# A semaphore for each part of a block's rows in the expert phase of a decoder step

## The reference, cut to what matters

```python
def expert_block(args):
    toks, e = args
    xb = x_pad[toks]
    hb = jax.nn.silu(xb @ w1[e]) * (xb @ w3[e])
    return hb @ w2[e]

out = lax.map(expert_block, (row_tok.reshape(n_blocks, EXPERT_BLOCK), block_expert))
```

## Time and profile before

| what | value |
| --- | --- |
| median of 3 runs | 2936.85 us (2933.5 to 2942.09) |
| the profiled execution | 2944.2 us, its span 2942.7 us |
| mean granted TensorE clock | 0.955 |
| TensorE busy | 2629.6 us, 89% of the span |
| HBM read, written | 460.86 MB, 112.29 MB |
| experts: first hidden product to last output product | about 1848 to 2848 us |

### The profile page before, as it was taken

One profiled execution on the slowest core, in us unless ns is written; L12 is line 12 of the kernel. 1 busy time (PEld: TensorE's weight loads), 2 busy tenths in 40 slices (PEclk: granted clock), 3 DMA queues, 4 the chain that ended last, 5 costly groups with the idle time before them and its releaser, 6 DMA issues. The chain is left out here.

```text
span 2942.7 us, 63889 instructions
## 1 busy us (share of the span) xinstructions
PE 2629.6 (89%) x23589; PEld 1367.6 (46%) x23589; DVE 1380.8 (47%) x2816; ACT 1049.8 (36%) x1938; POOL 646.5 (22%) x914
## 2 busy tenths in 40 slices
PE   7999999976988898998989997788889997788888
PEld 3444444433544444554535554454445554454443
DVE  2241414143877787887867776122222221122218
ACT  2222222113777777777842221211111211111114
POOL 0101010101112111211201223333233332233343
PEclk8999999997999999999999998899999999899989
DMA  8020201146667676766763344887977879979737
GB/s 321 15 86 15 83 17 67 47 150 221 212 223 265 224 245 222 253 214 227 249 224 104 129 145 150 247 259 224 292 224 219 245 232 322 308 215 277 240 110 316
DMA packets 296450, 576.79 MB, mean 196 GB/s; under 512 B 79766, under 2 KB 96215, under 8 KB 292236
## 3 DMA queue, kind: packets, MB, share of 16 engines
q1 hardware_dynamic: 194472, 427.99, 44.0%
q0 software_dynamic: 101440, 145.99, 16.6%
q10 hardware_dynamic: 324, 0.10, 0.0%
HBM read 460.86 MB, written 112.29 MB: 195 GB/s over the span
## 5 line engine op out<-in xcount | busy, mean ns | idle before, releaser
L1253 DVE TENSOR_TENSOR_SCAN left<-leave,left 128x512 f32<-128x512 f32 (+3 forms) x320 | 358.5, 1120 | 137.1 <-ACT leave L1135 136.3
L442 PE MATMUL bank<-xnT,w_in 128*128 128x512 f32 x768 | 330.3, 592 | 0.0
L1937 POOL DMA_DIRECT2D rowsP<-xs_d x324 | 214.6, 670 | 472.0 <-issue 386.0
L2036 DVE TENSOR_TENSOR sg<-sg,bank 128x128 f32<-128x128 f32 x160 | 46.0, 288 | 565.4 <-ACT sg L1973 565.4
L1996 PE MATMUL bank<-w,o_sq 128*32 128x256 f32 x3840 | 233.0, 404 | 73.2 <-DVE o_sq L2031 73.2
L2003 PE MATMUL bank<-w,hT 128*32 128x256 f32 x5120 | 296.4, 380 | 0.3 <-issue 0.3
L1056 POOL DMA_DIRECT2D w_out<-in_cache_v x256 | 137.4, 537 | 662.9 <-issue 658.1
L1973 ACT ACTIVATE sg<-bank 128x128 f32<-128x128 f32 x160 | 44.4, 277 | 548.9 <-PE bank L1996 548.9
L1996 PE MATMUL bank<-oT,o_sq 128*32 128x256 f32 x3712 | 211.9, 386 | 25.0 <-DVE o_sq L2031 23.7
L1620 PE MATMUL bank<-w_out,w 128*128 128x512 f32 x512 | 229.4, 601 | 2.8 <-DVE w L1684 2.8
L442 PEld LDWEIGHTS bank<-xnT,w_in 128*128 128x128 f32 x768 | 145.6, 190 | 181.8 <-issue 179.4
(11 more groups left out here) (408 smaller groups left out, 3373.7 us busy)
## 6 DMA issues: line engine op xcount, KB each, us to landing
w_out<-in_cache_v POOLq DMA_DIRECT2D x256, 256.0 KB
w_out<-in_cache_k SPq DMA_DIRECT2D x256, 256.0 KB
w<-in_w SPq DMA_DIRECT2D x128, 512.0 KB, 15.3
w<-in_w SPq DMA_DIRECT2D x22, 2048.0 KB, 18.3
oT<-in_w SPq DMA_DIRECT2D x22, 2048.0 KB, 19.2
w_out<-in_w SPq DMA_DIRECT2D x20, 2048.0 KB, 19.0
ys_d<-zeros SPq DMA_DIRECT2D x32, 816.0 KB
ys_d<-y POOLq DMA_DIRECT2D x166, 128.0 KB, 7.5
```

Of the source, the lines that this page charges most:

```text
L442: mm = pe.matmul(ps[:, :], w, m, start=(i == 0), stop=(i == len(parts) - 1))
L1253: dve.tensor_tensor_scan(left[n % 4][:, 0:cols][:, ::-1], leave[n % 4][:, 0:cols][:, ::-1], leave[n % 4][:, 0:cols][:, ::-1], left[n % 4][ ...
L1937: pool.dma_start(x_in[64 * half:64 * half + 64, ds(n & 1, 1), u * (XW // 2):(u + 1) * (XW // 2)].rearrange("p a n -> p (a n)"), in_strips( ...
```

## The change

The one semaphore `in` becomes four, one for each of the four transfers (unit and half) of a block. ACT and SP wait for all four. POOL no longer waits at the end of a body; instead each of the next block's four transfers waits, just before it is issued, until the transfer of the same part of the block before has landed. So that the counts need no special case, four transfers of row 0 are issued before `placed`, whose data is overwritten. The number of blocks and the offset of the next expert are read inside the body, after the four loads and before the store, in every block.

```diff
-    s = {n: k.sem(f"p7_{n}") for n in ("in", "cp", "xT", "h0", "h1", "sg", "hT", "y", "ye", "sp")}
+    s = {n: k.sem(f"p7_{n}") for n in ("cp", "xT", "h0", "h1", "sg", "hT", "y", "ye", "sp")}
+    PARTS = [(u, half) for u in range(UNITS) for half in range(2)]
+    s_in = [k.sem(f"p7_in_u{u}_h{half}") for u, half in PARTS]
...
         sp.wait_ge(sems["placed"], 1)
-        sp.wait_ge(s["in"], 64)
+        for landed in s_in:
+            sp.wait_ge(landed, 32)
...
     def gpsimd(pool):
-        pool.nop().then_inc(s["ye"], 2)
-        pool.nop().then_inc(s["cp"], 2)
-        pool.wait_ge(sems["placed"], 1)
+        def part(buffer, row, u, half):
+            return pool.dma_start(x_in[64 * half:64 * half + 64, buffer, u * (XW // 2):(u + 1) * (XW // 2)].rearrange("p a n -> p (a n)"),
+                                  in_strips(io[f"xs_d{half}"], row, u))
+
         def load(n, row):
             hold(pool, s["cp"], n + 1, s["sp"])
-            for u in range(UNITS):
-                for half in range(2):
-                    pool.dma_start(...).then_inc(s["in"], 16)
+            for at, (u, half) in enumerate(PARTS):
+                hold(pool, s_in[at], 16 * n + 16, s["sp"])
+                part(ds(n & 1, 1), row, u, half).then_inc(s_in[at], 16)
...
-        def before(e):
-            return pool.value_load(keep["offs"][0:1, e:e + 1], min_val=0, max_val=G)
-
-        def body(n, e, b, offs):
-            load(n, pool.snap(e * CAP + offs + b * G))
-            store(n)
-            hold(pool, s["in"], 64 * n + 64, s["sp"])
-
-        n = experts(pool, body, before)
+        def numbers(e):
+            return blocks_of(pool, e), pool.value_load(keep["offs"][0:1, e:e + 1], min_val=0, max_val=G)
+
+        pool.nop().then_inc(s["ye"], 2)
+        pool.nop().then_inc(s["cp"], 2)
+        for at, (u, half) in enumerate(PARTS):
+            part(slice(0, 1), 0, u, half).then_inc(s_in[at], 16)
+        pool.wait_ge(sems["placed"], 1)
+        count = pool.alloc_register("blocks_loaded")
+        pool.reg_mov(count, 0)
+        following = numbers(0)
+        for e in range(NE):
+            blocks, offs = following
+            with pool.Fori(0, blocks) as b:
+                n = pool.snap(count, min_val=0, max_val=MAX_BLOCKS)
+                load(n, pool.snap(e * CAP + offs + b * G))
+                if e + 1 < NE:
+                    following = numbers(e + 1)
+                store(n)
+                pool.reg_add(count, count, 1)
+        n = pool.snap(count, min_val=NE, max_val=MAX_BLOCKS)
         load(n, 0)
         store(n)
         store(n + 1)
-        hold(pool, s["in"], 64 * n + 64, s["sp"])
+        for landed in s_in:
+            hold(pool, landed, 16 * n + 32, s["sp"])
...
         def landed(n):
-            act.wait_ge(s["in"], 64 * n + 64)
+            for part in s_in:
+                act.wait_ge(part, 16 * n + 32)
```

More of the change, by code:

```diff
@@ L1929, in gpsimd @@
     def gpsimd(pool):
-        pool.nop().then_inc(s["ye"], 2)
-        pool.nop().then_inc(s["cp"], 2)
-        pool.wait_ge(sems["placed"], 1)
+        def part(buffer, row, u, half):
+            return pool.dma_start(x_in[64 * half:64 * half + 64, buffer, u * (XW // 2):(u + 1) * (XW // 2)].rearrange("p a n -> p (a n)"),
+                                  in_strips(io[f"xs_d{half}"], row, u))
         def load(n, row):
             hold(pool, s["cp"], n + 1, s["sp"])
-            for u in range(UNITS):
-                for half in range(2):
-                    pool.dma_start(x_in[64 * half:64 * half + 64, ds(n & 1, 1), u * (XW // 2):(u + 1) * (XW // 2)].rearrange("p a n -> p (a n)"),
-                                   in_strips(io[f"xs_d{half}"], row, u)).then_inc(s["in"], 16)
+            for at, (u, half) in enumerate(PARTS):
+                hold(pool, s_in[at], 16 * n + 16, s["sp"])
+                part(ds(n & 1, 1), row, u, half).then_inc(s_in[at], 16)
         def store(n):
```

## The result

| | median of 3 runs | range | span of the profiled execution |
| --- | --- | --- | --- |
| before | 2936.85 us | 2933.5 to 2942.09 | 2942.7 us |
| changed | 2830.73 us | 2830.22 to 2831.98 | 2829.2 us |

The ratio is 0.9637, 95% interval 0.9614 to 0.9661: 106 us less by the medians. The forecast was 2849, range 2815 to 2912.

What follows compares the result with a forecast made beforehand. Rows landing late among weights, with one load in flight, bound the expert stage; 163 us removable less 18, 23, 15, 2 and 17 left 88 us, giving 2849 us as a median, range 2815 to 2912.

Steps and rivals of the forecast that it cites:

- A wait for each part: POOL's row loads: each part reissued on its own landing, cycle 9.0 to 11.0 us against 13.6 and 14.7.
- The first rival: Row loads: all four parts land together, so only turnaround is won, 2887 us; chance 0.22.
- last part's remaining excess: Late blocks: the last part's cycle still exceeds a block's by 0.6 us, 39 times, 23 us kept.
- Turnaround: POOL, landing to next issue: saves 0.6 us within an expert and 1.7 us at its first block.
- The thirtieth transfer: POOL's stall every 30 transfers moves to a load's second part; 1 us for each of 16, 15 us in all.
- The slower rival: The thirtieth transfer's stall holds parts 1 to 3 inside a load, uncushioned 2977 us; chance 0.05.
- The store behind the parts: POOL's queue: stores wait behind held parts, covered because a store lands within 13.4 us and two blocks are 21 us.
- The full stretch: 2430 to 2550 us, single-block experts, DMA already full: 18 us, half of its 36, stays held by weights.
- slower weights: Expert stage: weights slow because rows come oftener, 17 us deducted, leaving the stage at 912 us.
- a bound of 888 us for DMA: Expert stage: 247 MB at 278 GB/s take 888 us, so at most 112 of 163 us can be won.
- the second rival: Expert stage: weights land after they are needed in more places, a third of the gain stays, 2907 us; chance 0.12.
- The fourth: Row loads: nothing changes, since an earlier issue only waits in DMA's own queue, 2937 us; chance 0.04.

Runs made afterwards that it cites:

- Thinned weights: Kernel before with three quarters of w1 and w3 of experts 1 to 31 left out: 2793.6 us; the changed kernel with the same edit: 2793.1 us.
- one gate: Changed kernel, but all four parts' semaphores are waited for before part 0 is issued: 2900.7 us, ratio 0.9879.
- with two: Changed kernel with parts waited for in pairs, both halves of a unit landing before either is issued again: 2848.9 us, ratio 0.9705.
- the loads spread: Changed kernel with each row transfer cut as one strip of 32 partitions with both units, still 64 KB: 2798.3 us, ratio 0.9548.
- Cutting it the other way: Kernel before with loads alone cut into strips of 32 partitions with both units, stores and semaphore as they were: 2794.6 us, ratio 0.9523.

## Why the prediction was right, and where its terms were off

**What bounds the kernel.** Right: rows among weights, one load in flight. Thinned weights remove nearly all of the lateness with the old code (12.7 us are left), and removing the lateness gives the clock back (31 us).

**A wait for each part.** Right as the main term, and the parts do land apart. The first rival (parts land together, 2887 us) describes what one gate gives, 2900.7, and that isn't what happened. The rule of the Trainium skill on the 16 counts did not decide: no part was held back to its block's last landing, and no run here reads the counts of single engines. A part's own cycle was put at 9.0 to 11.0 us, from landings of 8.2 and 10.2. The landings came out longer: 9.2 us in the median over the stage, and 8.7 to 11.7 for the four parts issued from 2498.85 on. The last part's remaining excess, put at 23 us, is the 9.7 us of waits that are left. So the landings were taken too short and the loss that follows from them too large, and that the two errors oppose each other is luck.

**Turnaround.** Its price was right in size: 50 us forecast for it with some clock, 37 measured, of which the reads are 20. But it doesn't add to the parts: with the parts apart the reads are worth nothing (2831.0 against 2830.7). The rest of the turnaround, the address computed ahead, was not tried by itself.

**The thirtieth transfer.** That the dummies shift it by four, onto the second part, was right for one semaphore. With four the period itself is another. The runs with one gate and with two show the stall every 26 or 27 transfers, at places that move through the block, at the same transfers in both. The price was off: 1 us each was taken, 15 us in all. With one gate a stall inside a load costs about 0.7 us, and one second store costs 3.5. In the changed kernel such stalls can't be told apart from the spacing of the loads; only second stores late by 0.7 to 1.2 us show, at four blocks. The slower rival asked for 6.4 us each and is out.

**The store behind the parts.** "Covered" was right for TensorE and not for ACT. Its result copies wait for a store's landing more than before, 13.6 us in 10 then, and by the waits of the changed kernel now:

```profile
ACT y L1995 <- DMA ys_d<-y: 76.6, 47, 2.6
```

At most 2.6 us each, and no product's wait is put down to ACT's copy: some of the cover is gone, and the rest holds.

**Dummies.** Wrong: "hidden". POOL's first real load waits for them, 3.7 us.

**Weights.** The full stretch was named as the place, with 18 us kept of its 36. It kept more: 22.0 us of waits and, at the two longest, hidden products of 9.50 and 8.90 us where 7.09 is normal, 4.2 us of clock. The timeline of PE:

```profile
2379.29 3.70 PE L2020 MATMUL bank<-w,hT 128*32 128x256 f32 x64
2396.22 9.50 PE L2013 MATMUL bank<-w_out,o_sq 128*32 128x256 f32 x128 [13.23 <-DMA w_out<-in_w]
2405.54 3.69 PE L2020 MATMUL bank<-w,hT 128*32 128x256 f32 x64
2414.49 8.90 PE L2013 MATMUL bank<-w,o_sq 128*32 128x256 f32 x128 [5.25 <-DMA w<-in_w]
```

The third wait, 3.5 us at 2461.69, lies in the same stretch (it is the 56th block, which before started at 2543.12). The 17 us kept elsewhere for slower weights were not needed: outside that stretch no product's wait is put down to them. The 17 went back to a bound of 888 us for DMA, and that step was wrong. The stage ended at 882 us, so that 118 us were won where at most 112 were held possible. The 278 GB/s behind the bound came from 7.5 us; the earlier trace rows already had 322 GB/s over 120 us with rows and weights, and with the loads spread most of the stage ran at 295.

**The sum.** The stage lost 118 us where 88 were forecast. The forecast kept 75 of the 163 removable; this is what each term came to: last part's excess 23, measured 9.7; full stretch 18, measured 26; thirtieth transfers 15, ACT's waits 2 and weights elsewhere 17, none of which is seen in front of a product; other clock, not charged, 7 (578.0 less the 567 of full speed, less the 4.2 above; 1.8 of it is the stage's first product, 8.92 us, and 1.7 the product behind the third wait for weights, 8.80). That is 43 kept and 120 removed, against 118. So the mechanism was right and the deductions were too large by some 30 us, above all the 17 for weights elsewhere and the 15 for the thirtieth transfers. From 118 in the stage 4.4 go back ahead of and behind it, which the forecast didn't have, and before's profiled execution lay 7.35 us above its median: 106.

**The other rivals.** Weights did become the largest loss that is left, but with 22.0 us in three waits, where the second rival (2907 us) stood 58 us above the forecast. The fourth, that an earlier issue only waits in DMA's queue, has at most a part: landings rose from 7.5 to 9.2 us in the median, and a cycle fell by more, from 13.6 to 10.4 and 11.7.

**What it missed.** I put the 8 to 10 us of a landing down as latency and asked only how to hide them. The experiments show that rows are late where two things meet, weights in flight and this cut of the transfers; take away either and nearly all of the lateness goes. Cutting it the other way takes 138 us from the kernel before, more than the change, which then adds nothing that can be measured (2798.3 us with it, 2794.6 without).

## What to carry to other kernels

When an engine that loads waits for all of a group and issues all of it again, the cycle is issue, landing and turnaround in a row; a semaphore for each member turns it into each member's own landing, and reading the counts ahead as well was then worth nothing. Before hiding a transfer's time, ask what it is made of: count the packets of its queue per transfer and look at the outermost size on both sides. And when such a stage is relieved, look for the one stretch where the next resource is already full; here a run of experts with one block each kept 26 us.

## What the hardware showed that I had not expected

A POOL transfer of 64 KB with an outer size of 2 on one side has 112 packets more, of 16 bytes each by the queue's bytes, than one with 32 on both sides. Among weights its landings of 9.2 us in the median became 6.4, and 5.3 with the stores cut likewise.

POOL stalls on its own queue at fixed numbers of its transfers. With one semaphore for the loads it is every 30th, and in the kernel before the profile names the rows' DMA as what ended it, 14 times, 81.6 us in all. With four semaphores it is every 26th or 27th: in the run with one gate the stalls stand at transfers 26, 52, 78, 105, 158, 184, 210 and so on, counted from the first load with the dummies left out. None shows between 105 and 158; one there would fall on a first store, which waits for other things anyway. One of them, before a fourth part:

```profile
2446.18 1.99 POOL L1934 DMA_DIRECT2D rowsP<-xs_d  x3 [7.79 <-DMA rowsP<-xs_d]
2448.82 0.65 POOL L1934 DMA_DIRECT2D rowsP<-xs_d  x1 [0.66 <-issue]
```

A landing of the transfer two back fits the kernel before, where that is the last part of the rows. It doesn't fit here, as two transfers back was issued less than 2 us earlier. What the stall waits for, and why its number changes with the semaphores, no run here tells.
